# Attention with the values held in TensorE, two heads' turned weights moving, and four sample pages side by side

## The chip, the cores and the metric

The kernel runs as one program on one NeuronCore of a Trainium2 chip. The metric is the device time of an execution in microseconds, as the median of three runs.

## The reference, cut to what matters

One layer of a decoder: a projection, two groups of eight attention heads side by side, an output projection and a SwiGLU block, for a prompt of 1024 tokens and eight samples that each have 4096 earlier tokens in pages of 128. What matters here is the attention of the prompt, and the stick-breaking attention of the samples:

```python
# group A, per head: three branches over the prompt, merged by gates
p = softmax(q @ kc.T * scale + mask_c); o_cmp = p @ vc        # 63 compressed keys
o_slc = softmax(q @ k_slc.T * scale + causal) @ v_slc         # with 1024 tokens every block is selected
o_win = softmax(q @ k_win.T * scale + window) @ v_win         # the last 512 tokens
o_nsa = gates[0] * o_cmp + gates[1] * o_slc + gates[2] * o_win
# group B, per head (the prompt, and each sample over its 4096 paged rows)
z = q @ k.T * scale
log_1m = where(mask, log_sigmoid(-z), 0)
suffix = reversed_cumsum(log_1m) - log_1m
o_sb = where(mask, exp(log_sigmoid(z) + suffix), 0) @ v
```

## The kernel before

The stages are `project`, `compress`, `attend`, `decode_nsa`, `mix_out` and `swiglu`, one after another with a barrier between some of them. The diff is in `attend` and in one constant.

`attend` is written out by hand for each engine. A step is one query tile of 128 rows (`t`, 0 to 7), one of two heads (`u`) and one kind: stick-breaking (`sb`), compressed (`cmp`), selected (`sel`) or window (`win`). A body holds two heads, 64 steps in the order u, t, kind. The body runs four times: once written out, twice in a register loop (`eng.Fori(1, 3)`), once written out. A step t of `sb` and `sel` covers t + 1 key tiles, `win` at most five, `cmp` one block of 63 keys.

For each step TensorE makes the scores into one of two score banks (L1115 to L1134). For the softmax kinds VectorE takes the row maximum (L1314) and ScalarE the exponential (L1241). For `sb` VectorE copies the scores (L1318), ScalarE makes the logarithm in three steps (L1250 to L1256), GpSimd the positive part (L1088), VectorE a reversed running sum (L1328), GpSimd a difference (L1091) and ScalarE the exponential (L1262). Two steps later TensorE turns the weights, 128 x 128 at a time, into two PSUM banks (L1153), VectorE and ScalarE copy the banks out in turn (L1225, L1227). Three steps later TensorE multiplies (L1170): the turned weights are the stationary operand, 128 columns, and 64 columns of values move, 65 for the softmax kinds, whose last column is ones, so that the sum of the weights comes out beside the product. VectorE then divides by that sum, multiplies by the gate and adds into `mix` (L1335 to L1350). In step s TensorE's queue holds the scores of s, the transposes of s - 2, the product of s - 3, then the work for the samples.

The samples' stick-breaking attention is spread between these steps. While one head is worked on, SP loads the 32 key pages of sample h (128 rows of 512 numbers each, L1012) into four slots, GpSimd multiplies them by the query (L1070) and VectorE sums each head's 64 products (L1377). Meanwhile SP loads the value pages of sample h - 1 into four slots (L1018, after a wait at L1017 for a slot to come free), and TensorE multiplies them (L1190): 8 columns of weights are stationary, the page's 512 columns move, and 32 pages add up in one bank. The last sample's value pages come after the last body. SP's queue alternates key page and value page.

## Time and profile before

| | us |
|---|---|
| median of three runs | 3199.31 (3196.07 to 3200.15) |
| the profiled execution | 3171.88 |
| its span, first to last instruction | 3169.9 |
| TensorE busy in the span | 2790.5 (88%) |
| VectorE, ScalarE, GpSimd busy | 1329.0, 825.6, 865.7 |
| mean granted clock of TensorE | 0.843 of 2.4 GHz |

The span holds all stages; the changed one is about a third of it. Engines work at the same time, so their busy times don't add up. The granted clock has two levels, 1.2 and 2.4 GHz, and a mean between them says how the time is shared out.

### The profile page before, as it was taken

What the parts mean: (1) busy time and instruction counts of PE and PEld (TensorE: products, weight loads), DVE (VectorE), ACT (ScalarE), POOL (GpSimd) and SP (SyncE); (2) the same over time, 40 slices, a digit from 0 to 9 for tenths busy, and PEclk for the clock granted to TensorE, in tenths of its full rate; (3) what the DMA queues carried; (4) which work ended last, traced back from release to release, by engine and by line L of the source; (5) the groups of instructions that cost most, each with busy time, mean ns of one, the idle gap of its engine ahead of it and who ended that gap; (6) DMA issues with size and microseconds to landing.
All of it is one profiled execution on the core that took longest, in us unless ns stands there. A gap on an engine that the chain in (4) does not pass through costs nothing. (4 is left out here: it accounts for less than half of the span.)

```text
span 3169.9 us, 48300 instructions
## 1 busy us (share of the span) xinstructions
PE 2790.5 (88%) x14396; PEld 2061.5 (65%) x14396; DVE 1329.0 (42%) x2664; ACT 825.6 (26%) x1540; POOL 865.7 (27%) x909
## 2 busy tenths in 40 slices
PE   7989698949999999999999715883989999999999
PEld 6868677736755555555555203442449999999999
DVE  3562233316565656556566223332431111114444
ACT  4232233313232333333333100110221111113333
POOL 0220344215464555445455103431200000000000
PEclk9999699975596977769798955555989999999999
DMA  4233744363355454445544411213112111113200
GB/s 144 87 114 117 179 124 130 83 111 101 90 167 137 150 147 135 140 139 155 146 140 151 133 22 44 67 45 128 67 63 65 46 46 46 46 43 99 67 31 23
DMA packets 265582, 314.41 MB, mean 99 GB/s; under 512 B 58326, under 2 KB 172815, under 8 KB 265207
## 3 DMA queue, kind: packets, MB, share of 16 engines
q1 hardware_dynamic: 248423, 271.20, 29.4%
q0 software_dynamic: 16576, 40.43, 5.2%
q8 instruction: 99, 1.62, 0.2%
q14 instruction: 132, 1.08, 0.1%
q10 hardware_dynamic: 352, 0.08, 0.0%
HBM read 278.89 MB, written 37.44 MB: 100 GB/s over the span
## 5 line engine op out<-in xcount | busy, mean ns | idle before, releaser
L1070 POOL TENSOR_TENSOR late<-late 128x512 f32<-128x512 f32 x256 | 335.8, 1314 | 255.0 <-DMA late<-in_cache_sb_kv 212.5
L2036 PE MATMUL pg<-h_turned_hi,w_gu_hi 128*128 128x344 f32 x1056 | 338.4, 320 | 9.9 <-DVE h_turned_lo L2084 9.9
L2038 PE MATMUL pg<-h_turned_hi,w_gu_lo 128*128 128x344 f32 x1056 | 338.3, 320 | 0.0
L2037 PE MATMUL pg<-h_turned_lo,w_gu_hi 128*128 128x344 f32 x1056 | 338.2, 320 | 0.0
L1190 PE MATMUL decode_ps<-late,weights_dec 128*8 128x512 f32 x512 | 308.0, 704 | 8.5 <-DMA late<-in_cache_sb_kv 6.8
L1241 ACT ACTIVATE probs<-scores,minus_max 128x63 f32<-128x63 f32 (+4 forms) x192 | 109.6, 571 | 591.6 <-DVE minus_max L1314 553.3
L2162 PE MATMUL py<-w_down_hi,act_hi 128*128 128x256 f32 x792 | 225.7, 285 | 9.9 <-DVE w_down_lo L2209 9.9
L2079 DVE TENSOR_TENSOR w_gu_lo<-late,w_gu_hi 128x512 fp32r<-128x512 f32 x88 | 60.9, 692 | 402.2 <-ACT w_gu_hi L2049 402.2
L2163 PE MATMUL py<-w_down_lo,act_hi 128*128 128x256 f32 x792 | 225.1, 284 | 0.0
L2164 PE MATMUL py<-w_down_hi,act_lo 128*128 128x256 f32 x792 | 225.0, 284 | 0.0
L2145 POOL DMA_DIRECT2D out_y_prompt<-y_rows x32 | 17.4, 545 | 745.8 <-DVE y_rows L2197 745.8
L2036 PEld LDWEIGHTS pg<-h_turned_hi,w_gu_hi 128*128 128x128 f32 x1056 | 199.5, 189 | 10.1 <-issue 9.9
L2038 PEld LDWEIGHTS pg<-h_turned_hi,w_gu_lo 128*128 128x128 f32 x1056 | 199.6, 189 | 0.0
L2037 PEld LDWEIGHTS pg<-h_turned_lo,w_gu_hi 128*128 128x128 f32 x1056 | 199.1, 189 | 0.0
L1170 PE MATMUL out_ps<-v_sel_win,probs_turned 128*128 128x65 f32 (+1 forms) x1056 | 178.6, 326 | 11.6 <-DVE mix L1348 10.8
L1170 PEld LDWEIGHTS out_ps<-v_sel_win,probs_turned 128*128 128x128 f32 x1056 | 170.9, 245 | 23.3 <-issue 21.4
L831 DVE TENSOR_TENSOR rows_turned_lo<-px_c,rows_turned_hi 128x256 fp32r<-128x256 f32 x264 | 99.7, 420 | 189.5 <-ACT rows_turned_hi L782 189.5
L1377 DVE TENSOR_REDUCE z_dec<-late 128x8 f32<-128x512 f32 x256 | 169.0, 673 | 5.2 <-POOL late L1070 5.1
L2204 DVE TENSOR_TENSOR act_lo<-swiglu_act,act_hi 128x1408 fp32r<-128x1408 f32 (+1 forms) x72 | 105.9, 1471 | 149.5 <-ACT act_hi L2181 149.5
L2049 ACT ACTIVATE w_gu_hi<-late 128x512 fp32r<-128x512 f32 x88 | 55.7, 633 | 417.4 <-PE pg L2038 410.1
L1614 POOL DMA_DIRECT2D kv_sel<-in_cache_nsa_kv x144 | 84.4, 586 | 279.6 <-issue 279.6
L2162 PEld LDWEIGHTS py<-w_down_hi,act_hi 128*128 128x128 f32 x792 | 153.0, 193 | 11.2 <-issue 11.2
(289 smaller groups left out, 5743.5 us busy)
## 6 DMA issues: line engine op xcount, KB each, us to landing
late<-in_cache_sb_kv SPq DMA_DIRECT2D x512, 256.0 KB, 2.9
late<-in_w_gate_up SPq DMA_DIRECT2D x88, 256.0 KB, 2.9
late<-in_cache_nsa_kv SPq DMA_DIRECT2D x160, 128.0 KB, 3.7
late<-in_cache_nsa_kv POOLq DMA_DIRECT2D x96, 128.0 KB, 3.4
late<-in_w_down SPq DMA_DIRECT2D x4, 2816.0 KB, 11.0
w_in_raw<-in_w_in SPq DMA_DIRECT2D x40, 256.0 KB, 4.9
kv_sel<-in_cache_nsa_kv POOLq DMA_DIRECT2D x144, 32.0 KB, 2.0
x_sb<-in_x_prompt SPq DMA_DIRECT2D x8, 512.0 KB, 4.1
```

What stands on the lines that cost most here:

```text
L1070: eng.tensor_tensor(prod[:, p % NPR], kr[:, p % RING], qb[:, u], ALU.mult).then_inc(multiplied, 1)
L1170: mm = eng.matmul(O[:, 0:HD if kind == "sb" else HD + 1], l, r, start=c == 0, stop=c == tiles - 1)
L1190: eng.matmul(DB[0:NH, :], aw[:, :, NPAGE - 1 - p], vr[:, p % RING], start=p == 0, stop=p == NPAGE - 1).then_inc(v_used, 1)
L1241: eng.activation(pr[:, s % 2, 0:w], S[:, s % 2, 0:w], ACT.Exp, bias=nm[:, s:s + 1]).then_inc(exp_done, 1)
L1377: eng.tensor_reduce(zd[:, u, :, NPAGE - 1 - p], prod[:, p % NPR].rearrange("p (h d) -> p h d", h=NH), AX.X, ALU.add).then_inc(reduced, 1)
L2036: eng.matmul(pg[:, e, c, 0:CW], w_hi[:, h, j, :], hT_hi[:, k, cols], start=k == 0, stop=False)
L2037: eng.matmul(pg[:, e, c, 0:CW], w_hi[:, h, j, :], hT_lo[:, k, cols], start=False, stop=False)
L2038: mm = eng.matmul(pg[:, e, c, 0:CW], w_lo[:, h, j, :], hT_hi[:, k, cols], start=False, stop=k == KT - 1)
L2162: eng.matmul(out, a_hi[:, h, j, :], wd_hi[:, f, :], start=f == 0, stop=False)
L2163: eng.matmul(out, a_hi[:, h, j, :], wd_lo[:, f, :], start=False, stop=False)
L2164: mm = eng.matmul(out, a_lo[:, h, j, :], wd_hi[:, f, :], start=False, stop=f == NF - 1)
L2204: eng.tensor_tensor(lo, src, hi.bitcast(F32), ALU.subtract).then_inc(a_lo_done, 1)
```

## The change

- **Products.** The values become the stationary operand (64 columns) and the turned weights move. For the softmax kinds the weights of two heads stand side by side in `prT`, 256 columns, because both heads share keys and values; for `sb` each head moves its own 128. Each product fills one of two column halves of TensorE and lands in PSUM partitions 0 to 63 or 64 to 127 of the bank `O`: selected and window, or the two `sb` heads, or two query tiles of `cmp`. A batch is such a pair; a block of 16 steps (two heads, two query tiles) has five, and the three larger kinds are issued in pieces over two or three steps (`PV_AT`).
- **Output.** The result stands with its columns in the partitions, so ScalarE copies it to `oT` (`copy_out`), TensorE turns it back into one of the two banks that the transposes use (`turn_back`), and VectorE scales and adds (`finish`). The sums of the weights come from ScalarE's exponential (`accum_out` into `den`) in place of the column of ones.
- **Bank copies.** VectorE copies every third bank, ScalarE the others.
- **Samples' values.** Eight slots in place of four. Four pages go one after another to four column groups of 32 (the weights padded with zeros to 32 columns) and to PSUM partitions 0, 32, 64 and 96; each group adds up eight pages, and a matmul with 128 ones adds the four. The weights are still ready one head later, but key and value pages are spread evenly by an estimate of each step's cost (`DEC`) over 288 slots in the one sequence, the last sample's values among them.
- **Order.** No register loop: 256 steps are written out, with two heads and two query tiles alternating in a block. Page numbers are read eight at a time. Queries are loaded per block, by GpSimd's queue, which also takes the loads of the `sb` values from SP.

```diff
-        vx = sb("v_sel_win", [P, 2, TILES, KVH, HD + 1])
...
+        vx = sb("v_sel_win", [P, 2, TILES, KVH, HD])
+        qn = sb("q_nsa_hi_twice", [P, 2, 2, 2 * P], F32R)
+        qs = sb("q_sb_hi_twice", [P, 2, 2, 2 * P], F32R)
+        qn_lo = sb("q_nsa_lo", [HD, 2, 2, 2 * P], F32R)
+        qs_lo = sb("q_sb_lo", [HD, 2, 2, 2 * P], F32R)
...
-        prT = sb("probs_turned", [P, 2, TILES, P])
-        fac = sb("factor", [P, 64, 2])
...
+        SB_SLOT, EVEN_SLOT, ODD_SLOT, CMP_SLOT, SLOTS = 0, 8, 20, 33, 35
+        prT = sb("probs_turned", [P, SLOTS, 2 * P])
+        fac = sb("factor", [P, 2, 4])
+        part = sb("out_parts", [P, 2, 2, HD])
...
+        vr_low = late[:, 2048:4096].rearrange("p (r n) -> p r n", r=VRING // 2)
+        vr_high = sb("value_pages_high", [P, VRING // 2, 512])
+        value_slot = lambda p: (vr_low, vr_high)[p % VRING // 4][:, p % 4]
...
-        aw = sb("weights_dec", [P, NH, NPAGE])
+        aw = sb("weights_dec", [P, 32, NPAGE])
...
+        BLOCK = [(0, 0, "sb"), (0, 0, "cmp"), (1, 0, "cmp"), (0, 1, "cmp"), (1, 0, "sb"), (1, 1, "cmp"), (0, 0, "sel"), (1, 0, "sel"),
+                 (0, 1, "sb"), (0, 0, "win"), (1, 0, "win"), (0, 1, "sel"), (1, 1, "sb"), (1, 1, "sel"), (0, 1, "win"), (1, 1, "win")]
+        STEPS = [(N, u, 2 * k + a, kind) for N in range(NBODY) for k in range(4) for u, a, kind in BLOCK]
...
+        NBATCH = 5 * U // 16
+        PV_AT, OUT_AT = ((8,), (10, 11), (12, 13, 14), (18, 19), (20, 21, 22)), (9, 12, 15, 20, 23)
+        END = U - 16 + OUT_AT[4] + 1
...
+        PT_USES = []
+        for i in range(END):
+            PT_USES += [("out", bt) for bt, _ in at_iteration(i, OUT_AT)]
+            if 2 <= i < U + 2:
+                PT_USES += [("group", b) for b in range(G0[i - 2], G0[i - 1])]
+        bank_of = {use: n % 2 for n, use in enumerate(PT_USES)}
+        use_before = {use: PT_USES[n - 2] for n, use in enumerate(PT_USES) if n >= 2}
+
+        cost = [0.9 + 0.4 * tiles_of(kind, t) for N, u, t, kind in STEPS]
+        DEC = [[] for _ in range(END)]
+        for n in range((NH + 1) * NPAGE):
+            goal, i, total = (n + 0.5) / ((NH + 1) * NPAGE) * sum(cost), 0, cost[0]
+            while total < goal:
+                i += 1
+                total += cost[i]
+            DEC[i].append((n // NPAGE, n % NPAGE))
+        VGROUP = {6: 0, 9: 1, 13: 2, 16: 3, 20: 4, 23: 5, 27: 6, 31: 7}
+        reduced_at = lambda s: [] if s == 0 else [s - 1] if s < NPAGE - 1 else [s - 1, s]
...
-                def value_page(b, p):
-                    if not (zero(b) and p < RING):
-                        eng.wait_ge(v_used, b * NPAGE + p - RING + 1)
-                    page = eng.value_load(pt[0:1, bass.ds(b * NPAGE + p, 1)], min_val=0, max_val=NPOOL - 1)
-                    eng.dma_start(vr[:, p % RING], io["cache_sb"][bass.ds(page * P, P), 1, :]).then_inc(v_loaded[p % RING], 16)
+                def value_page(b, p, page):
+                    if b or p >= VRING:
+                        eng.wait_ge(v_used, b * NPAGE + p - VRING + 1)
+                    eng.dma_start(value_slot(p), io["cache_sb"][bass.ds(page * P, P), 1, :]).then_inc(v_loaded[p % VRING], 16)
...
+                def load_queries(blk, n):
+                    N, k = blk // 4, blk % 4
+                    dst, name, t = ((qs[0:HD], "T_hi", T_QS), (qs[HD:P], "T_hi", T_QS), (qs_lo, "T_lo", T_QS),
+                                    (qn[0:HD], "T_hi", T_QN), (qn[HD:P], "T_hi", T_QN), (qn_lo, "T_lo", T_QN))[n]
+                    src = turned_rows[name][:, t + 2 * N:t + 2 * N + 2, 2 * P * k:2 * P * (k + 1)]
+                    eng.dma_start(dst[:, blk % 2], src).then_inc(q_blocks[blk % 2], 16)
+
+                def load_keys(N):
+                    for rows, name in ((slice(0, HD), "T_hi"), (slice(HD, P), "T_lo")):
+                        eng.dma_start(ks[rows], turned_rows[name][:, T_KB + 2 * N:T_KB + 2 * N + 2, :]).then_inc(ks_loaded, 16)
+
+                def load_values(N):
+                    v = io["sb_p"].rearrange("(t p) (c h d) -> c p t h d", p=P, c=2, h=NH)[1]
+                    for u in range(2):
+                        eng.dma_start(vs[:, u], v[:, :, 2 * N + u, :]).then_inc(vs_loaded, 16)
...
+                def bank_free(use):
+                    if use in use_before:
+                        what, n = use_before[use]
+                        if what == "out":
+                            eng.wait_ge(out_done, n + 1)
                         else:
+                            eng.wait_ge(saved[saver(n)], saves(n + 1)[saver(n)])
...
+                def turn_back(bt):
+                    N, t, kind, W = batch(bt)
+                    eng.wait_ge(ot_saved, bt + 1)
+                    bank_free(("out", bt))
+                    for u in range(W // P):
+                        mm = eng.transpose(PT[:, bank_of["out", bt], u * P:(u + 1) * P], oT[:, bt % 2, u * P:(u + 1) * P], ident[:, :])
+                    mm.then_inc(out_turned, 1)
...
-                    for c in range(tiles):
-                        if kind == "cmp":
-                            l, r = prT[0:NCP, m % 2, 0, :], vcp[0:NCP, bass.ds(kv, 1), :].rearrange("p o d -> p (o d)")
-                        elif kind == "sb":
-                            l, r = prT[:, m % 2, c, :], vs[:, u, c, :]
-                        else:
-                            l, r = prT[:, m % 2, c, :], vx[:, 0 if kind == "sel" else 1, lo + c, bass.ds(kv, 1), :].rearrange("p o d -> p (o d)")
-                        mm = eng.matmul(O[:, 0:HD if kind == "sb" else HD + 1], l, r, start=c == 0, stop=c == tiles - 1)
-                    mm.then_inc(pv_done, 1)
...
+                def product(bt, piece):
+                    N, t, kind, W = batch(bt)
+                    kv, pieces = N // 2, len(PV_AT[bt % 5])
+                    if piece == 0:
+                        by_v, by_a = saves(groups_ready(bt))
+                        eng.wait_ge(saved[0], by_v)
+                        eng.wait_ge(saved[1], by_a)
+                        if bt:
+                            eng.wait_ge(ot_saved, bt)
+                        if kind == "sb":
+                            eng.wait_ge(vs_loaded, 32 * (N + 1))
+                    if kind == "cmp":
+                        for z in range(2):
+                            mm = eng.matmul(O[HD * z:HD * z + HD, 0:W], vcp[0:NCP, kv, 0:HD], prT[0:NCP, CMP_SLOT + z, :], start=True, stop=True)
+                        mm.then_inc(pv_done, 1)
+                        return
+                    count = (t + 1, t + 1 if kind == "sb" else tiles_of("win", t))
+                    for c in range((t + 1) * piece // pieces, (t + 1) * (piece + 1) // pieces):
+                        for z in range(2):
+                            if c >= count[z]:
+                                continue
+                            if kind == "sb":
+                                l, r = vs[:, z, c, :], prT[:, SB_SLOT + c, z * P:z * P + P]
+                            else:
+                                name = ("sel", "win")[z]
+                                l, r = vx[:, z, first_tile(name, t) + c, kv, :], prT[:, slot_of(name, t) + c, :]
+                            mm = eng.matmul(O[HD * z:HD * z + HD, 0:W], l, r, start=c == 0, stop=c == count[z] - 1)
+                    if piece == pieces - 1:
+                        mm.then_inc(pv_done, 1)
...
-                            eng.matmul(DB[0:NH, :], aw[:, :, NPAGE - 1 - p], vr[:, p % RING], start=p == 0, stop=p == NPAGE - 1).then_inc(v_used, 1)
...
+                    if 1 <= h <= NH and s in VGROUP:
+                        pages = [SIDE * VGROUP[s] + i for i in range(SIDE)]
+                        if pages[0] == 0:
+                            eng.wait_ge(weights_done, h)
+                        for p in pages:
+                            eng.wait_ge(v_loaded[p % VRING], h * VPER - VPER + 16 * (p // VRING) + 16)
+                        for i, p in enumerate(pages):
+                            eng.matmul(DB[32 * i:32 * i + 32, :], aw[:, :, NPAGE - 1 - p], value_slot(p), start=p < SIDE, stop=p >= NPAGE - SIDE).then_inc(v_used, 1)
...
+                for i in range(END):
+                    if i < U:
+                        scores(i)
+                    for bt, _ in at_iteration(i, OUT_AT):
+                        turn_back(bt)
+                    if 2 <= i < U + 2:
+                        transposes(i - 2)
+                    for bt, piece in at_iteration(i, PV_AT):
+                        product(bt, piece)
+                    for h, s in DEC[i]:
+                        sample(h, s)
...
+                def copy_out(bt):
+                    N, t, kind, W = batch(bt)
+                    eng.wait_ge(pv_done, bt + 1)
+                    if bt >= 2:
+                        eng.wait_ge(out_turned, bt - 1)
+                    eng.activation(oT[:, bt % 2, 0:W], O[:, 0:W], ACT.Copy).then_inc(ot_saved, 1)
+
...
-                    f, f2 = fac[:, m % U, 0:1], fac[:, m % U, 1:2]
-                    eng.reciprocal(f, O[:, HD:HD + 1])
-                    eng.drain()
-                    eng.tensor_tensor(f2, f, gates[:, t, bass.ds(h * 3 + br, 1)], ALU.mult)
-                    eng.drain()
-                    if kind == "cmp" and t == 0:
-                        eng.tensor_tensor(f2, f2, rowok[:, :], ALU.mult)
-                    mx = mix[:, t, bass.ds(h * HD, HD)]
-                    if kind == "cmp":
-                        eng.tensor_scalar(mx, o, f2, None, ALU.mult).then_inc(out_done, 1)
-                    else:
-                        eng.scalar_tensor_tensor(mx, o, f2, mx, ALU.mult, ALU.add).then_inc(out_done, 1)
...
+                def finish(bt):
+                    N, t, kind, W = batch(bt)
+                    bank = PT[:, bank_of["out", bt], 0:W]
                     if kind == "sb":
+                        eng.wait_ge(out_turned, bt + 1)
+                        eng.tensor_copy(mix[:, t, 512 + 2 * N * HD:512 + 2 * N * HD + P], bank).then_inc(out_done, 1)
                         return
+                    f4 = fac[:, bt % 2, :].rearrange("p (a b) -> p a b", a=2)
+                    eng.wait_ge(out_turned, bt + 1)
+                    if kind == "cmp":
+                        eng.reciprocal(f4, den[:, t:t + 2, :, 0])
                         eng.drain()
+                        eng.tensor_tensor(f4, f4, gates[:, t:t + 2, 6 * N:6 * N + 6:3], ALU.mult)
+                        eng.drain()
+                        if t == 0:
+                            eng.tensor_scalar(f4[:, 0, :], f4[:, 0, :], rowok[:, 0:1], None, ALU.mult)
+                            eng.drain()
+                        out = mix[:, t:t + 2, 2 * N * HD:2 * N * HD + P].rearrange("p t (u d) -> p t u d", u=2)
+                        src = bank.rearrange("p (u t d) -> p t u d", u=2, t=2)
+                        eng.tensor_tensor(out, src, f4.unsqueeze(3).broadcast_to([P, 2, 2, HD]), ALU.mult).then_inc(out_done, 1)
+                        return
+                    eng.reciprocal(f4, den[:, t, :, 1:3])
+                    eng.drain()
+                    eng.tensor_tensor(f4, f4, gates[:, t, 6 * N:6 * N + 6].rearrange("p (u b) -> p u b", u=2)[:, :, 1:3], ALU.mult)
+                    eng.drain()
+                    src = bank.rearrange("p (u b d) -> p u b d", u=2, b=2)
+                    eng.tensor_tensor(part[:, :, :, :], src, f4.unsqueeze(3).broadcast_to([P, 2, 2, HD]), ALU.mult).then_inc(out_done, 1)
+                    eng.drain()
+                    mx = mix[:, t, 2 * N * HD:2 * N * HD + P].rearrange("p (u d) -> p u d", u=2)
+                    for z in range(2):
+                        eng.tensor_tensor(mx, mx, part[:, :, z, :], ALU.add)
```

## Rows read from the trace of the kernel before

**Rows 1.** The page, the granted clock of TensorE in 40 slices, in tenths
```profile
PEclk9999699975596977769798955555989999999999
```

**Rows 2.** Busy time by stretch: PE, weight loads, VectorE, ScalarE, GpSimd, granted clock, DMA
```profile
715.00:865.00 150.00, 143.82 (x514) 105.55 (x514) 89.99 (x208) 48.71 (x97) 75.25 (x61) 0.50 0.29 86
890.00:960.00 70.00, 69.26 (x345) 38.61 (x344) 49.67 (x97) 28.41 (x43) 44.51 (x29) 1.00 0.59 174
965.00:1009.00 44.00, 43.19 (x132) 25.06 (x131) 20.48 (x60) 10.75 (x29) 14.31 (x17) 0.50 0.43 112
715.00:1770.00 1055.00, 1021.19 (x4185) 596.06 (x4185) 652.54 (x1445) 358.67 (x662) 550.46 (x432) 0.77 0.48 137
...
1770.00:1816.00 46.00, 36.63 (x72) 5.05 (x70) 1.32 (x3) 0.42 (x1) 0.00 (x0) 0.93 0.53 160
```

**Rows 3.** PE's waits in 715 to 1770 us: total, times, longest
```profile
PE turned_ps L1153 <- ACT probs L1241: 16.1, 13, 4.9
```

**Rows 4.** Busy by stretch (PE, weight loads): L1170 alone, then L1190 alone
```profile
715.00:1770.00 1055.00, 304.10 (x1760) 285.54 (x1760) 0.77 0.48 137
...
715.00:1770.00 1055.00, 274.19 (x448) 27.86 (x448) 0.77 0.48 137
```

**Rows 5.** PE's timeline at granted clock 1.00: start, duration of the run, count
```profile
1196.40 1.89 PE L1190 MATMUL decode_ps<-late,weights_dec 128*8 128x512 f32 x4
1198.22 0.29 PE L1115 MATMUL scores<-kc_prompt_hi,q_nsa_hi_twice 64*128 x1
...
1198.71 0.85 PE L1153 MATMUL turned_ps<-ident,stick_weights 128*128 128x128 f32 x6
1199.40 1.23 PE L1170 MATMUL out_ps<-v_sel_win,probs_turned 128*128 x10
1200.56 1.03 PE L1190 MATMUL decode_ps<-late,weights_dec 128*8 128x512 f32 x2
```

**Rows 6.** PE's timeline at granted clock 0.50
```profile
871.35 0.96 PE L1170 MATMUL out_ps<-v_sel_win,probs_turned 128*128 128x65 f32 x4
872.23 1.88 PE L1190 MATMUL decode_ps<-late,weights_dec 128*8 128x512 f32 x2
874.04 0.69 PE L1131 MATMUL scores<-kT_sel_win,q_nsa_hi_twice 128*128 128x384 f32 x1
```

**Rows 7.** PE's timeline before 965 us; in brackets the idle time before
```profile
962.92 0.76 PE L1153 MATMUL turned_ps<-ident,probs 128*128 128x128 f32 x5 [1.03 <-ACT probs L1241]
```

**Rows 8.** VectorE by line, 715 to 1770 us; the last row by shape
```profile
L1341 DVE TENSOR_TENSOR factor<-factor,gates 128x1 f32<-128x1 f32 x192 | 82.1, 428 | 26.9 <-issue 19.7
L1225 DVE COPY probs_turned<-turned_ps 128x512 f32<-128x512 f32 (+4 forms) x176 | 79.0, 449 | 9.7 <-PE turned_ps L1153 9.6
...
L1335 DVE COPY mix<-out_ps 128x64 f32 (+1 forms) x63 | 14.0, 223 | 32.1 <-PE out_ps L1170 31.1
...
L1374 DVE TENSOR_TENSOR logw_dec<-z_dec,decode_ps 128x256 f32<-128x256 f32 x7 | 2.9, 421 | 8.1 <-PE decode_ps L1184 8.1
```

**Rows 9.** ScalarE by line and shape, 715 to 1770 us
```profile
L1227 ACT ACTIVATE probs_turned<-turned_ps 128x256 f32<-128x256 f32 x32 | 12.1, 378 | 0.6
```

**Rows 10.** GpSimd by line, 715 to 1770 us
```profile
L1070 POOL TENSOR_TENSOR late<-late 128x512 f32<-128x512 f32 x256 | 335.8, 1314 | 255.0 <-DMA late<-in_cache_sb_kv 212.5 <-DVE z_dec L1377 40.8 <-issue 0.9
L1088 POOL TENSOR_SCALAR late<-late 128x128 f32<-128x128 f32 (+3 forms) x64 | 105.2, 1643 | 36.1 <-DVE late L1318 36.1
L1091 POOL TENSOR_TENSOR late<-late 128x128 f32<-128x128 f32 (+3 forms) x64 | 89.7, 1402 | 234.2 <-DVE late L1328 234.2
L1056 POOL DMA_DIRECT2D q_sb_hi_twice<-scratch_T_hi x12 | 7.0, 580 | 0.0
```

**Rows 11.** Line L997: count, duration in ns (least, median, most), first and last start
```profile
L997 SPq DMA_DIRECT2D v_sel_win<-out_nsa_p x2: 628/8348/16067, 677.3 to 686.1; - x2
```

**Rows 12.** SP's own waits, 715 to 1820 us
```profile
SPq L1017 <- PE decode_ps L1190: 365.6, 133, 21.3
```

**Rows 13.** Line L1170, the same columns as rows 11
```profile
L1170 PE MATMUL out_ps<-v_sb,probs_turned x576: 222/275/447, 730.1 to 1769.8; 128*128 128x64 f32 x192
```

More of the change, by code:

```diff
@@ L974, in attend @@
-        zero = lambda N: isinstance(N, int) and N == 0
-        def turns(eng, body, tail):
-            body(0, 0)
-            with eng.Fori(1, 3) as i:
-                body(i, i - 1)
-            body(3, 1)
-            for s in range(H):
-                tail(s)
+        for m in range(U):
+            N, u, t, kind = STEPS[front_of(m)]
+            G0.append(G0[-1] + (tiles_of(kind, t) + 3) // 4)
+        saver = lambda b: 0 if b % 3 == 2 else 1
+        saves = lambda b: (b // 3, b - b // 3)
@@ L1037, in tail @@
-                def tail(s):
-                    value_page(NH - 1, s)
-                    if s == 5:
-                        store_row(NH - 2)
-                turns(eng, body, tail)
+                    eng.dma_start(io["osb_s"][b:b + 1, :], orow).then_inc(row_stored, 16)
+                for h in range(NH + 1):
+                    for p0 in range(0, NPAGE, 8):
+                        key_ids = numbers(h, p0) if h < NH else None
+                        value_ids = numbers(h - 1, p0) if h else None
+                        for p in range(p0, p0 + 8):
+                            if h < NH:
+                                key_page(h, p, key_ids[p - p0])
+                            if h:
+                                value_page(h - 1, p, value_ids[p - p0])
+                            if p == 5 and h >= 2:
+                                store_row(h - 2)
@@ L1125, in scores @@
                         e = min(w, a + 512)
-                        if kind == "sb":
-                            k = ks[:, u, a:e]
-                        else:
-                            k = kT[:, 0 if kind == "sel" else 1, bass.ds(kv, 1), lo * P + a:lo * P + e].rearrange("p o c -> p (o c)")
-                        own = [x for x in edges if a <= x[0] < e]
-                        eng.matmul(S[:, s % 2, a:e], q, k, start=True, stop=False)
-                        mm = eng.matmul(S[:, s % 2, a:e], q_lo, k[0:HD], start=False, stop=not own)
@@ L1133, in scores @@
-                        for z, (at, m) in enumerate(own):
-                            mm = eng.matmul(S[:, s % 2, at:at + P], identb[:, :], masks[:, m, :], start=False, stop=z == len(own) - 1)
-                    mm.then_inc(qk_done, 1)
-                def transposes(N, m):
-                    u, t, kind, lo, tiles = BACK[m % U]
+                        k = ks[:, u, a:e] if kind == "sb" else kT[:, 0 if kind == "sel" else 1, kv, lo * P + a:lo * P + e]
+                        own = [x for x in edges if a <= x[0] < e]
@@ L1146, in transposes @@
-                    for b in range(first, G0[m % U + 1]):
-                        if not (zero(N) and b < 2 and m >= 0):
-                            eng.wait_ge(saved[b % 2], N * (G // 2) + (base + b) // 2)
-                        if kind == "cmp":
-                            eng.sem_inc(steps, 1)
-                        for c in range(4 * (b - first), min(tiles, 4 * (b - first) + 4)):
-                            w = min(P, width(BACK[m % U]) - c * P)
-                            mm = eng.transpose(PT[0:w, b % 2, (c % 4) * P:(c % 4 + 1) * P], src[:, c * P:c * P + w], ident[:, :])
-                        mm.then_inc(turned, 1)
@@ L1192, in body @@
-                def body(N, kv):
-                    for s in range(U):
-                        scores(N, kv, s)
-                        kvb = lambda m: kv if m >= 0 else (1 if isinstance(N, int) else 0)
-                        if not (zero(N) and s < 2):
-                            transposes(N, s - 2)
-                        if not (zero(N) and s < 3):
-                            product(N, kvb(s - 3), s - 3)
-                        sample(N * 2 + s // H, s % H)
-                def tail(s):
-                    if s < 2:
-                        transposes(4, s - 2)
-                    if s < 3:
-                        product(4, 1, s - 3)
-                    sample(NH, s)
```

464 lines of the change are left out of this document (224 added, 240 removed).

## The prediction, on record before the change was run

> **What bounds the kernel now.** I read the page first: its row of the granted clock falls to half in the middle of the span [rows 1]. The change touches one stage, `attend`, so everything else keeps its time. The view by stretches shows that stage: work runs from 715 to 1770 us, and a tail of 46 us follows in which only TensorE and transfers are left [rows 2]. In the 1055 us of the body PE is busy 1021, VectorE 653, GpSimd 550, ScalarE 359, so PE sets the pace. The waits confirm it: PE's own longest comes to 16 us in 13 times [rows 3]. A microsecond of PE work taken out of the body is therefore worth about a microsecond, until another engine takes over.
>
> Two lines hold half of that work [rows 4]. The products (L1170) are busy 304 us in 1760 instructions; a run's last instruction overlaps what follows by some 0.07 us (1.23 recorded, 1.16 to the next start [rows 5]), and with about 256 runs that leaves 286. The sample's value pages (L1190) are busy 274 in the body; less 10 for the same reason leaves 264. The other lines and 34 us of idleness are 1055 - 286 - 264 = 505, so 471 of work.
>
> The clock is the second thing to read. In [rows 2] the stretches 715 to 865 and 965 to 1009 run at 0.50 (1.2 GHz) although PE is busy 96% and 98% of them; 890 to 960 runs at 1.00 (2.4 GHz), and the tail has 0.93 on average, although PE is busy only 37 of its 46 us. Prices at both levels come from the timeline, from one start to the next. At 2.4 GHz [rows 5]: a value matmul of 512 columns (1198.22 - 1196.40) / 4 = 0.455 us, a product of 65 columns 1.16 / 10 = 0.116, a transpose 0.69 / 6 = 0.115. At 1.2 GHz [rows 6]: 1.81 / 2 = 0.905 and 0.88 / 4 = 0.22. At 2.4 GHz throughout, the products would be 1760 x 0.116 = 204 and the body's pages 448 x 0.455 = 204. They took 550 for 408, so the mix of clocks now costs a factor of 1.35, and the other 471 are 348 at 2.4 GHz.
>
> **The change, part by part.**
>
> *Products.* Now the turned weights are loaded (128 columns) and 64 or 65 columns of values move. After it 64 columns of values are loaded and 256 columns (two heads) or 128 move. An fp32 matmul is two instructions (880 calls, 1760 rows). The new ones: compressed 16 batches x 2 x 2 = 64 of 256 columns; stick-breaking 36 tiles x 4 pairs x 2 heads x 2 = 576 of 128; selected 36 x 4 x 2 = 288 and window 30 x 4 x 2 = 240 of 256. By columns from the 512-column row, 256 cost 0.227 and 128 cost 0.114: 14.5 + 65.7 + 65.4 + 54.5 = 200. So streamed one after another the new products cost what the old ones do, 204. All of the gain hangs on the two column halves running at the same time. No matmul of this trace writes another part of the columns than the first, so the price lies between 200 and, with each pair at the cost of its longer half, 7 + 33 + 65 = 105. I take 105.
>
> *Value pages.* 512 instructions of 0.455 are 233 one after another. Four pages side by side could take a quarter, 58. But a page's second instruction has the page's own columns and must follow its first; in the order written, page 2's first can run beside page 1's second, and so on, so four pages take 5 steps for 8: 64 x 5 x 0.455 = 146. I take that. By the Trainium skill (TensorEngine Tiling (Array Packing), Theoretical Speedup), a dimension of up to 32 gives up to four times, which is the 58 and would make the result some 110 us lower; no row here shows either.
>
> *Turning back.* 128 new transposes x 0.115 = 15.
>
> *Unchanged*: 348 at 2.4 GHz. The tail of 46 us goes, because the pages of the last sample are now spread over the whole body; their work is in the 146.
>
> So PE's work at 2.4 GHz is 105 + 146 + 15 + 348 = 614, against 204 + 233 + 348 = 785 now; without any overlap it is 200 + 233 + 15 + 348 = 796.
>
> *The clock after.* The factor can be 1.0, or stay at 1.35, or reach 1.95 (0.22 / 0.116 and 0.905 / 0.455 average to that) if 2.4 GHz is never granted. The slow stretch 715 to 865 is the one almost without pages, where short products fill PE; the tail kept 2.4 GHz on long matmuls with gaps. The change turns 1760 short instructions into 1168 long ones, which speaks for a smaller factor. Against it, the clock fell at 965 right after PE had waited 1.03 us for ScalarE [rows 7], and a faster PE waits more. I take 1.25: 614 x 1.25 = 768.
>
> *Waits.* The 34 us of idleness stay. New ones: each of the 80 batches goes PE, ScalarE copy, PE turn, VectorE, and the turned block shares two PSUM banks with the transposes, so these queue behind `finish`. That chain is 0.38 (a 256-column copy on ScalarE [rows 9]) + 0.23 (two turns) + 0.16, 0.43 and 0.42 on VectorE (reciprocal, a one-column multiply, a 256-column multiply out of PSUM [rows 8]) = 1.6 us, of which the scores and products in between hide some. Between 0 and 80 x 1.6 = 128 I take 0.5 each: 40.
>
> *The other engines.* VectorE loses the five lines of the old output step (182 us in all, 82 of them the one-column multiply that takes 0.43 on average [rows 8]) and a third of its 79 us of bank copies, and gains about 93 (48 reciprocals and multiplies, 48 products of 128x256, 64 additions, 32 copies): 653 - 182 - 26 + 93 = 538. ScalarE gains 59 bank copies and 80 of `copy_out`: 359 + 54 = 413. GpSimd keeps 336 of key products and 195 of L1088 and L1091, and issues 102 loads at about 0.58: 590 [rows 10]. The eight value loads, moved to its queue from SP's, have many short rows; the same shape of issue took 0.6 to 16 us on SP [rows 11], so at worst they add 128 there. All stay below 842, so they cost nothing by themselves, but GpSimd no longer has half its time free. SP waited 366 us for the value matmuls to free a slot [rows 12]; eight slots in place of four, freed by fours, leave it as far ahead, so I cost it at nothing. Register instructions go with the loop; they run ahead of a busy PE, nothing.
>
> *Sum.* 768 + 34 + 40 = 842 from 715 to the end of the stage, where it was 1055 + 46 + 1 = 1102: 260 less. The profiled execution took 3171.9, 27 below the median of 3199.3. 3172 - 260 = 2912, and 2939 as a median: **2940 us**.
>
> **Rivals.**
>
> *PE near full clock.* Factor 1.0: 614 + 74 = 688, 414 less, 2785. For it: the long instructions. Against it: GpSimd's 590 and VectorE's 538 in strict order would then nearly pace it.
>
> *Each change between whole and divided columns empties the array.* There are 176 product pieces and 64 page groups, so 480 changes. A product of 64 columns is recorded at 0.275 [rows 13] where the next starts after 0.116; the 0.16 between is what an empty array would show. 480 x 0.16 = 77, so 919, and 3016. For it: the pieces are short, one to three per block and batch. Against it: no row, since nothing divides columns now. The Trainium skill (TensorEngine Tiling (Array Packing), Key Properties) states that changing the tiling mode drains TensorE; by that rule this rival holds.
>
> *The halves do not run together (the other side).* Place: products and pages. The work is then 796, above the 785 of now. At today's factor it is 796 x 1.35 + 74 = 1149, 47 more: 3246; at 1.25 it is 1069, 33 less: 3166. At 1.35 it decides as soon as overlap hides under 35 of the 433 us, since (1102 - 74) / 1.35 = 761. For it: the two instructions of one call always follow each other, and moving data for two halves must be read at once. Against it: nothing in the trace. This is also the case in which the change does not do what it says.
>
> *The clock stays at 1.2 GHz.* 614 x 1.95 + 74 = 1271, 169 more: 3368. For it: 715 to 865. Against it: every later stretch with pages comes back to 2.4 GHz.
>
> **How the numbers follow.** Forecast (overlap, factor 1.15 to 1.35, own range 2880 to 3000) 0.42; emptied array 0.16; near full clock 0.17; no overlap 0.18, of which a third is still faster; half clock 0.07. Faster by over 0.2%, about what a measurement of this kernel tells from no change: 0.42 + 0.16 + 0.17 + 0.06 = 0.81; within it 0.03; slower 0.16. The range of 2785 to 3200 leaves out the half clock, the slower part of no overlap and a little below: 0.2.
>
> **What would show it.** Right: two product matmuls of one piece starting within 0.02 us of each other or at half their stream; pages at some 2.3 us per group of four at 2.4 GHz; the body ending near 1557 with no tail; PE's granted clock above 0.8 there. Wrong: page instructions still 0.45 apart (no overlap); gaps of 0.1 to 0.2 us at the edges of each piece (emptying); 0.50 over long stretches; long PE waits for VectorE or ScalarE at the transposes after `turn_back`, or GpSimd busy over 90%, which would put the chain in place of PE's work.

## The result, and the profile after

| | before | after |
|---|---|---|
| median of four runs each | 3197.69 us | 3082.79 us (3075.28 to 3089.52) |
| ratio to before, 95% interval | | 0.9646 (0.9615 to 0.9677) |
| profiled execution | 3171.9 us | 3089.5 us |
| first to last matmul of `attend` | 714.5 to 1816.2, 1102 us | 703.7 to 1730.5, 1027 us |
| PE idle in it, mean granted clock | 43 us, 0.77 | 165 us, 0.67 |

The kernel is 3.5% faster: 115 us, where 260 were forecast. The two profiled executions are only 82 us apart, since that of the kernel before was 26 us below its median and that of the changed kernel 7 us above. Outside the stage the time changed by 8 us: the stage begins 11 us earlier, and what follows it takes 3 us longer. The clock row of the profile's page shows where to look:

```profile
PEclk9999799985567667667567655556999999999999
```

Where [rows 1] had 6 to 9 in the middle of the stage, this row has 5 to 7. The view by stretches (columns as in [rows 2]), the whole stage first and then its parts:

```profile
705.00:1730.00 1025.00, 860.20 (x3789) 456.64 (x3788) 574.61 (x985) 413.04 (x994) 576.39 (x486) 0.67 0.50 149
...
705.00:841.00 136.00, 116.89 (x412) 65.53 (x411) 81.19 (x151) 56.51 (x158) 91.11 (x85) 0.50 0.44 127
841.00:1400.00 559.00, 464.99 (x2132) 245.60 (x2132) 327.72 (x553) 229.09 (x545) 341.38 (x287) 0.71 0.56 168
1400.00:1730.00 330.00, 278.32 (x1248) 145.51 (x1247) 165.70 (x282) 127.44 (x291) 143.91 (x115) 0.68 0.43 127
```

PE is busy 860 us where it was 1058, and its clock is lower. Busy time times the mean clock is an estimate of the work in microseconds at 2.4 GHz: 860 x 0.67 = 576 against 1058 x 0.77 = 815. So some 239 us of work are gone, more than the forecast's 171. What answers to [rows 4], products (L1224) and pages (L1245):

```profile
L1224 PE MATMUL out_ps<-probs_turned,v_sel_win 128*64 128x256 f32 x528 | 105.7, 503 | 0.0
L1224 PE MATMUL out_ps<-probs_turned,v_sb 128*64 128x128 f32 x576 | 67.6, 387 | 1.1 <-issue 0.7 <-ACT probs_turned L1277 0.2
L1245 PE MATMUL decode_ps<-value_pages_high,weights_dec 128*32 128x512 f32 x256 | 57.9, 993 | 0.0
L1245 PE MATMUL decode_ps<-late,weights_dec 128*32 128x512 f32 x256 | 50.9, 878 | 0.0
```

The timeline at 2.4 GHz, which answers to [rows 5], shows how:

```profile
1132.45 1.08 PE L1224 MATMUL out_ps<-probs_turned,v_sel_win 128*64 128x256 f32 x8
...
1133.47 0.50 PE L1160 MATMUL scores<-kT_sel_win,q_nsa_hi_twice 128*128 128x512 f32 x1
...
1136.35 1.12 PE L1245 MATMUL decode_ps<-value_pages_high,weights_dec 128*32 128x512 f32 x8
...
1137.40 0.49 PE L1160 MATMUL scores<-kT_sel_win,q_nsa_hi_twice 128*128 128x512 f32 x1
```

Eight product instructions of 256 columns take 1.02 us, 0.128 each, where one after another at the 0.227 of the forecast would be 1.82. Eight page instructions take 1.05, 0.13 each for 0.455: the four pages run side by side, and both instructions of a call do. What PE waited for, against the single row in [rows 3]:

```profile
PE turned_ps L1187 <- DVE out_parts L1416: 81.9, 28, 8.6
PE turned_ps L1195 <- ACT late L1320: 24.9, 25, 3.4
PE decode_ps L1236 <- ACT late L1334: 18.9, 7, 5.4
PE turned_ps L1187 <- DVE mix L1409: 12.2, 13, 2.0
```

Three of these four rows are the new chain: turned output, `finish`, a bank free again. Its longest wait in the timelines of three engines:

```profile
1138.78 2.02 DVE L1388 TENSOR_TENSOR_SCAN late<-late 128x896 f32<-128x896 f32 x1 [2.36 <-ACT late L1308]
...
1139.35 0.60 PE L1187 MATMUL turned_ps<-ident,probs 128*128 128x128 f32 x4
...
1140.72 1.85 DVE L1449 TENSOR_REDUCE z_dec<-late 128x8 f32<-128x512 f32 x3
1142.49 1.08 DVE L1373 TENSOR_REDUCE minus_max<-scores 128x1 f32<-128x896 f32 x1
...
1143.41 2.08 POOL L1122 TENSOR_TENSOR late<-late 128x896 f32<-128x896 f32 x1
...
1143.73 4.22 DVE L1413 TENSOR_TENSOR factor<-factor,gates 128x4 f32<-128x4 f32 x1
...
1145.44 2.48 POOL L1096 TENSOR_TENSOR late<-late 128x512 f32<-128x512 f32 x2
...
1148.02 0.42 DVE L1416 TENSOR_TENSOR out_parts<-turned_ps,factor 128x256 f32<-128x256 f32 x1
1148.50 0.90 PE L1187 MATMUL turned_ps<-ident,probs 128*128 128x128 f32 x3 [8.55 <-DVE out_parts L1416]
```

VectorE takes 4.22 us to multiply four columns, and ends as GpSimd's three tensor instructions end (1143.41 to 1147.92). PE waits 8.55 us for the bank behind it. The first 3.5 us of that wait lie ahead of `finish`, while VectorE works through a scan, three reductions and a row maximum.

### The profile page after: what moved, and what is told of

The parts are those of the page before. It is cut to its first block and busy times, and to the rows that moved or that the text cites. A ratio compares the mean times of both kernels' runs of the same rounds, so it can differ in the third digit from the quotient of the medians.

```text
span 3087.5 us, 43599 instructions
## 1 busy us (share of the span) xinstructions
PE 2598.0 (84%) x13932; PEld 1918.4 (62%) x13932; DVE 1250.4 (40%) x2201; ACT 879.9 (28%) x1871; POOL 891.7 (29%) x957
## 5 line engine op out<-in xcount | busy, mean ns | idle before, releaser
L1096 POOL TENSOR_TENSOR late<-late 128x512 f32<-128x512 f32 x256 | 322.6, 1269 | 142.9 <-DVE z_dec L1449 93.4
L1187 PE MATMUL turned_ps<-ident,probs 128*128 128x128 f32 (+1 forms) x592 | 143.2, 361 | 100.4 <-DVE out_parts L1416 81.9
L1292 ACT ACTIVATE probs<-scores,minus_max 128x63 f32<-128x63 f32 (+8 forms) x192 | 109.7, 571 | 394.6 <-DVE minus_max L1373 381.4
L1373 DVE TENSOR_REDUCE minus_max<-scores 128x1 f32<-128x63 f32 (+8 forms) x192 | 103.6, 540 | 181.0 <-PE scores L1163 144.3
L1187 PEld LDWEIGHTS turned_ps<-ident,probs 128*128 128x128 f32 (+1 forms) x592 | 93.1, 183 | 111.6 <-DVE out_parts L1416 74.6
L736 PE MATMUL ph_c<-rows_turned_hi,w_cmp_hi 128*128 128x512 f32 (+1 forms) x288 | 125.9, 437 | 37.6 <-DVE rows_turned_lo L829 37.6
```

The costliest lines, as they stand in the source:

```text
L736: eng.matmul(out, w1_hi[:, kk, half, jj, :], x_hi, start=step == 0, stop=False)
L1096: eng.tensor_tensor(prod[:, p % NPR], kr[:, p % RING], qb[:, h % 2], ALU.mult).then_inc(multiplied, 1)
L1187: mm = eng.transpose(PT[0:w, bank, (c % 4) * P:(c % 4 + 1) * P], src[:, c * P:c * P + w], ident[:, :])
L1292: eng.activation(pr[:, f % 2, 0:w], S[:, f % 2, 0:w], ACT.Exp, bias=nm[:, f % 8:f % 8 + 1], accum_out=den[:, t, u, br:br + 1]).then_inc(ex ...
```

## The experiments

Two things had moved: the clock (0.77 to 0.67) and the idle time (43 to 165 us). **Theory A**: the waits pull the clock down, so taking waits away gives both back. **Theory B**: the clock follows how much work the array has; the change took work away and the clock went with it. Theories C and D stand in the expectations. Each ratio is to the kernel before on the same chip. The other columns are from one profiled execution: the stage goes from the first to the last matmul of `attend`, and PE's busy time is taken over whole microseconds, so that a row can miss its stage by 1 or 2 us.

| kernel | stage us | PE busy | PE idle | clock | ratio (95%) |
|---|---|---|---|---|---|
| before | 1102 | 1058 | 43 | 0.77 | 1 |
| after | 1027 | 860 | 165 | 0.67 | 0.9646 (0.9615 to 0.9677) |
| after, no gate multiply | 989 | 855 | 133 | 0.68 | 0.9594 (0.9536 to 0.9653) |
| after, factors on GpSimd | 996 | 860 | 134 | 0.66 | 0.9605 (0.9545 to 0.9665) |
| after, pages in turn | 1093 | 931 | 161 | 0.80 | 0.9918 (0.9890 to 0.9946) |
| after, halves in turn | 1016 | 856 | 159 | 0.68 | 0.9694 (0.9636 to 0.9751) |
| after, one dense matmul a step | 1011 | 841 | 169 | 0.76 | 0.9641 (0.9593 to 0.9688) |
| after, three | 1035 | 884 | 151 | 0.85 | 0.9682 (0.9635 to 0.9729) |
| factors on GpSimd, one dense | 992 | 836 | 155 | 0.76 | 0.9548 (0.9502 to 0.9593) |
| the same, dense in the waits | 998 | 846 | 151 | 0.78 | 0.9579 (0.9527 to 0.9630) |
| before, one dense | 1052 | 1007 | 44 | 0.86 | 0.9755 (0.9709 to 0.9801) |
| before, pages alone, ring of 4 | 1282 | 1156 | 125 | 0.51 | 1.0488 (1.0441 to 1.0534) |
| the same, three dense | 1229 | 1008 | 220 | 0.78 | 1.0356 (1.0304 to 1.0409) |
| before, pages alone, ring of 8 | 1180 | 1145 | 34 | 0.51 | 1.0161 (1.0093 to 1.0229) |
| the same, one dense | 1125 | 1048 | 76 | 0.63 | 0.9956 (0.9920 to 0.9992) |
| the same, two dense | 1063 | 964 | 98 | 0.77 | 0.9824 (0.9747 to 0.9901) |

**Fewer waits.** The first run drops the multiply by the gates, here and in the branch for `cmp`; its outputs lack the gates:

```diff
                     eng.reciprocal(f4, den[:, t, :, 1:3])
                     eng.drain()
-                    eng.tensor_tensor(f4, f4, gates[...][:, :, 1:3], ALU.mult)
-                    eng.drain()
```

> Leaves out the multiplication of the reciprocal by the gates in finish (48 of VectorE's small SBUF-to-SBUF multiplies, 49 us busy, up to 4.2 us each); the outputs lack the gates. Theory A (PE's waits pull the clock down): the 94 us that PE waits for VectorE at the two shared banks fall to about 40, the stage's mean granted clock rises from 0.67 to 0.72 or more, and the time falls by 100 to 130 us. Theory B (the clock follows how much long streaming work PE has, not the waits): the waits fall the same way, the clock stays at 0.67, and the time falls by 30 to 50 us.

The second keeps the result and makes the factor on GpSimd, a step ahead:

```diff
+                    eng.tensor_tensor(f4, d4, minus1[...], ALU.pow)
+                    eng.drain()
+                    mm = eng.tensor_tensor(f4, f4, g4, ALU.mult)
```

> GpSimd works out gate / sum for a batch one step before VectorE needs it (a power of -1 and a multiply on 4 columns), so finish is one multiply out of PSUM before the bank is free; same results. Theory A: waits at the banks fall by 50 or more, the clock rises to 0.72 or more, 80 to 130 us faster than the changed kernel. Theory B: 30 to 50 us faster at a clock of 0.67.

The bank wait halves in both (81.9 to 41.6 and 42.3). This is its row without the multiply:

```profile
PE turned_ps L1187 <- DVE out_parts L1412: 41.6, 19, 4.3
```

In the whole stage 31 us of idleness went, and the clock stayed (0.68, 0.66) where theory A had 0.72 or more. By the ratios 0.5 and 0.4 points came back, about 15 us each, but the intervals overlap that of the change, so this gain is not shown. Theory A falls.

**The parts of the overlap.** Pages of a group one after another in the same 32 columns:

```diff
-    eng.matmul(DB[32 * i:32 * i + 32, :], aw[:, :, NPAGE - 1 - p], value_slot(p), ...)
+    eng.matmul(DB[0:32, :], aw[:, :, NPAGE - 1 - p], value_slot(p), ...)
```

> Puts the four value pages of a group back into one column group, one after another; all else as in the changed kernel. Their work at 2.4 GHz goes from 68 to 233 us. Theory A: the clock stays near 0.67 and the time rises by 165 x 1.54 = 254, less some 30 of waits that the longer work covers: 200 to 250 us. Theory B: the long work brings the clock back to 0.75 or above in the stage and the time rises by 100 us or less.

```profile
704.00:1796.00 1092.00, 931.19 (x3791) 447.12 (x3791) 566.28 (x985) 411.15 (x994) 576.21 (x486) 0.80 0.46 140
```

The pages cost 0.45 each again, 512 x (0.45 - 0.13) = 164 us more work at 2.4 GHz, but the stage is only 66 us longer: the clock rose to 0.80 with 161 us of waits still there. It is also the change without its pages, and gains 0.8%.

Halves of a product one after the other:

```diff
-    for c in range(...):
-        for z in range(2):
+    for z in range(2):
+        for c in range(...):
```

> Issues each piece's matmuls for the first column half, then those for the second, where the changed kernel alternates; the same instructions and results, but only neighbours at the turn can overlap. Work at 2.4 GHz rises by 26 (stick-breaking) and up to 40 (window) us. Theory A: 66 x 1.54 = 100 us slower at most, 60 to 100. Theory B: the clock rises a little with it, 20 to 50 us slower. If the halves hardly overlapped in the first place, no change.

No difference beyond the intervals. The records show why: the second half starts beside the first all the same, and a 256-column product averages 0.15 us at 2.4 GHz in both kernels (128 columns: 0.091 for 0.069).

**Useless work.** If B is right, work that nobody uses must raise the clock and cost little. One dense matmul (the whole array, 512 columns) ahead of each step's scores, into the bank that they overwrite; then three, by `range(3)`:

```diff
+    for z in range(1):
+        eng.matmul(S[:, f % 2, 0:512], identb[:, :], cmask[...], start=True, stop=True)
```

> The changed kernel with one more matmul in each of the 256 steps of the stage, ahead of the step's scores: 512 columns of 16-bit values over the whole array, into the bank that the scores then overwrite. It computes nothing that is used. One costs about 0.22 us at 2.4 GHz and 0.43 at 1.2, by the scores of 512 columns, 56 or 110 us in all. Theory B (the granted clock of the stage follows how much the array streams; the three cheaper parts took work away and with it the clock): the stage's mean granted clock rises from 0.67 to about 0.71, which gives back most of the price: stage 1020 to 1050 us against 1022, ratio 0.962 to 0.975 against the changed kernel's 0.965. Theory C (the clock is set by something that the added work doesn't change, the breaks between short batches, say): the clock stays at 0.67, the 56 us cost 84, stage about 1106, ratio 0.99.

> As the run with one dense matmul per step, with three of them: 168 us of work at 2.4 GHz that is not used. Theory B: the clock rises to about 0.80, as it did with the pages in turn, and the stage takes about 1090 us (744 us of work over 0.80, and 160 idle), ratio 0.985 to 0.995. Theory C: the clock stays at 0.67, 250 us more, stage about 1270 us, ratio 1.04.

With three, by stretches:

```profile
701.00:1736.00 1035.00, 884.06 (x4560) 445.78 (x4560) 564.59 (x985) 410.73 (x994) 576.26 (x486) 0.85 0.50 148
```

For 56 and 168 us of added work, one costs nothing that can be measured and three about 0.4 points, with intervals that overlap; the clock rose to 0.76 and 0.85. Theory C had 0.99 and 1.04. The waits did not go (169 and 151 us), so they are not what holds the clock. The same single matmul in the kernel before:

> The kernel before, with one dense matmul ahead of each step's scores and nothing else. Theory B: its clock rises from 0.77 to about 0.85, 815 us of work and 56 more over 0.85 is 1025, with 43 idle a stage of 1068 against 1102, ratio 0.99. Theory C: clock 0.77, 56 us cost 73, ratio 1.02.

```profile
715.00:1766.00 1051.00, 1006.99 (x4434) 573.53 (x4510) 642.21 (x1448) 359.56 (x664) 552.27 (x432) 0.86 0.51 144
```

56 us of work that computes nothing made the stage 50 us shorter and the kernel 2.4% faster, more than the expected 1%.

**The pages alone.** The kernel before, with four pages side by side and nothing else of the change:

```diff
+    for p in range(b, b + 4):
+        eng.matmul(DB[32 * (p - b):32 * (p - b) + 32, :], aw[:, :, NPAGE - 1 - p], vr[:, p % RING], ...)
```

> The kernel before with one part of the change alone: four value pages of a sample in a row, each in its own 32 columns of the array, on the same ring of four pages; the prompt's attention, its order and its loads as before. The products keep 64 or 65 columns over the whole array. The pages' work falls from 307 us by about 220. Theory B: the clock of the stage falls from 0.77 to about 0.67 as in the changed kernel, since as much work has gone; busy time 1058 x 0.77 = 815 us less 236 is 579, over 0.67 is 864, with 34 to 80 us idle a stage of 900 to 945 us against 1102, ratio 0.937 to 0.951: no slower than the whole change, which would mean that the rest of the change gained nothing. Theory C (the changed kernel's short batches and their waits brought the clock down): the clock stays at 0.77 here, 579 / 0.77 = 752, stage 790 to 830 us, ratio 0.90 to 0.915.

> The kernel before with the pages side by side alone, and three dense matmuls ahead of each step's scores, 168 us of work at 2.4 GHz that nothing uses. Theory B (the pages alone were slower than before only because the clock fell to 1.2 GHz, 98% of the stage): the clock comes back to about 0.85; 588 us of work and 168 more over 0.85 is 889, with 100 to 125 us idle a stage of about 1000 us, ratio 0.96 to 0.975, faster with the useless work than without by some 280 us. Rival D (the page's waits for their data or the blocked load queue made it slow): the clock stays near 0.51 and the stage grows by 330 us, ratio 1.15.

Both forecasts missed: 4.9% slower at 0.51, and with the clock brought back to 0.78 still 3.6% slower. So the clock was not all of it. GpSimd's wait for key pages pointed to the ring of four: SP holds one queue, and key pages stood in it behind value pages that waited for a whole group to be used. That row with the ring of four:

```profile
POOL late L1068 <- DMA late<-in_cache_sb_kv: 477.5, 139, 34.6
```

With the ring of eight of the change added:

> The kernel before with the pages side by side, and now also with the ring of eight value pages of the changed kernel; the prompt's attention as before. In the run without the larger ring GpSimd waited 478 us for key pages, which stood on the load queue behind value pages that waited for their slots (212 us in the kernel before). If both that and the clock made it slow, the two part here. The late keys gone: PE idle falls from 125 us to 40 to 80. The clock: theory B gives 579 us of work (815 less 236) over a clock that follows the streaming; at 0.67 as in the changed kernel 864, stage 905 to 945, ratio 0.937 to 0.951; at 0.51 as in the run with the small ring 1135, stage about 1190, ratio 1.025. Products of 64 columns over the whole array are shorter than those of the changed kernel, so the lower clock is the likelier, 0.55 to 0.6, ratio about 1.0.

```profile
POOL late L1071 <- DMA late<-in_cache_sb_kv: 40.5, 4, 32.6
...
713.00:1892.00 1179.00, 1145.40 (x4256) 788.17 (x4256) 643.70 (x1448) 358.39 (x663) 538.53 (x432) 0.51 0.43 129
```

The late keys are gone (478 to 41 us) and PE is busy 97% of the stage. With 34 us of waits left and about 230 us less work at 2.4 GHz the stage is 78 us longer, because it ran at 1.2 GHz for 98% of its time. It also limits theory B: 1145 x 0.51 = 584 us of work is as much as the changed kernel's 576, which ran at 0.67, so the amount of work alone does not set the clock. Giving work back:

> As the run before it, with one dense matmul ahead of each step's scores, 56 us at 2.4 GHz. Theory B: the clock comes back to 0.70 to 0.75: 635 us of work over it is 850 to 907, with 50 idle a stage of 900 to 960, ratio 0.937 to 0.955, which would be no slower than the whole change. If the rest of the change (values stationary, the unrolled order) is what made it faster: the ratio stays at 1.0 or above.

> As the run before it with two dense matmuls per step, 112 us. Theory B: clock about 0.80, 691 us over it is 864 and 50 idle, stage about 915, ratio 0.94.

The clock came up more slowly than expected (0.63, in a profiled execution 19 us above its median, and 0.77), and idle time with it (76, 98), so 0.9956 and 0.9824 stand for the forecast 0.95 and 0.94. B's direction held, its sizes did not. With two useless matmuls a step to bring back the clock of the kernel before, pages side by side are worth 1.8%; one useless matmul without them gave 2.4%, and the intervals overlap. The change with its pages in turn gains 0.8%, so neither half reaches the change's 3.5% by itself. How the rest divides over the products, the order of the steps and the loads is not shown; no run takes these apart.

**Both remedies together.** The factors on GpSimd and one dense matmul per step; then two matmuls behind the scores, ahead of the bank wait, in the 160 narrow steps:

```diff
                     mm.then_inc(qk_done, 1)
+                    dense(f)
...
+                    a = 512 if width(kind, t) <= 512 else 1024
+                    for z in range(2 if a == 512 else 0):
+                        eng.matmul(S[:, f % 2, a:1024], identb[:, :], cmask[...], start=True, stop=True)
```

> The run with the factors on GpSimd, and one dense matmul ahead of each step's scores as in that run. Theory B (the clock follows how much the array streams, and waits are paid beside it): both gains add: 573 us of work and 56 more over a clock of 0.755, 134 us idle, stage about 967 us, ratio about 0.951. Theory C (the clock isn't changed by added work) is refuted by now; if the gains don't add (the fewer waits and the higher clock buy the same thing), ratio 0.96.

> As the run before it, but with the dense matmuls behind the step's scores, ahead of the point where TensorE waits for the bank of the turned weights, and only in the 160 steps whose scores fill one bank: two each, into the other bank, 70 us at 2.4 GHz. Theory B: the clock rises to about 0.78, and part of the added work lies in time that was idle: 643 us over 0.78 is 824, with 110 to 134 idle a stage of 935 to 960 us, ratio 0.942 to 0.950. If place does not matter: as the run before it, 0.951; if only the wide steps need the work, the clock stays near 0.70 and the ratio is 0.97.

The first is the best kernel of the study, 0.9548, and its interval lies below that of the change. That it beats the factors alone (0.9605) is not shown: the intervals overlap, and the stage is 992 against 996. Work put ahead of the wait did not shorten it (idle 151).

## Why the prediction failed

In its own terms, the stage was to be 614 x 1.25 + 74 = 842. With the products and pages that the trace shows, and the prediction's 15 and 348 kept, the work is 128 + 68 + 15 + 348 = 559; busy time over it is 860 / 559 = 1.54, and 559 x 1.54 + 165 = 1026. From 842: work -55 x 1.25 = -69; clock 559 x 0.29 = +162; waits +91.

*The clock factor is the step that failed.* The prediction took 1.25, below today's 1.35, because "1760 short instructions" became "1168 long ones". It had the other reading in front of it: the stretch "almost without pages" of [rows 2] ran at 0.50 with PE busy 96%. The pages' long matmuls were the work that held the clock up, and the change took 70% of it out (233 to 68 us at 2.4 GHz). Putting them back in turn raised 0.67 to 0.80, and the runs with the pages alone made the whole stage like that stretch, 0.51. The rival "the clock stays at 1.2 GHz" had 0.07; it was the neighbour of what happened (66% of the stage at 1.2 GHz, before 46%). The Trainium skill (TensorE: Matmul & The Clock Gate, Part 1: The HAM clock gate) says that "the default state is throttled, and activity releases the throttle"; these runs agree, with 0.67, 0.76 and 0.85 for none, one and three useless matmuls. But a busy PE was not enough: with the pages alone and the ring of eight it was busy from 1579.1 to 1741.8 us, 163 us without a break, at 1.2 GHz. What exactly the clock follows stays open: 164 us of pages in turn gave 0.80, 168 us of matmuls spread over all steps 0.85, and nearly equal work ran at 0.67 and 0.51.

*Waits, second.* 40 were allowed for the new chain between 0 and 128. The rows for the turned banks shown above, with 3.3 from a smaller one, give 81.9 + 24.9 + 12.2 + 3.3 = 122, near the upper bound. The mis-sized term is the small multiply: 0.43 a piece from [rows 8], measured 1.24 on average (0.16 to 4.22). Taking it away halved the bank wait. For part of what is left the sum has no term: `finish` queues behind VectorE's other work, 3.5 us of it in the longest wait shown above.

*Work.* Pages: 146 forecast, 68 measured. The "5 steps for 8" were wrong; a page's second instruction does not hold up the other pages, and a group takes 1.05 us where 2.3 were named. Products: 105 forecast, 128 measured (528 instructions at 0.15, 576 at 0.069, 64 at 0.145). So the -55 is -78 and +23, two errors that partly cancel. The two halves start 0.007 us apart and a pair of 256 columns takes 0.21, so the overlap is as forecast; the rest is the next point.

*The array emptied at each change* was given 0.16 as a rival of its own. It happens, at a smaller price. In the records at 2.4 GHz a transpose takes 0.109 from start to start within a run and 0.203 as the last ahead of a product (in the kernel before, where products use all columns, 0.109 there too; these are medians). The last instruction of a pair of 256 columns takes 0.209 ahead of the next pair and 0.309 ahead of whole-array work. So a change costs 0.09 to 0.10, not 0.16: 480 changes are some 48 us, partly within the 128 and 68 above, and more than paid for by the pages. The Trainium skill (TensorEngine Tiling (Array Packing), Key Properties) says that changing the tiling mode drains TensorE; the trace agrees, with 0.09 to 0.10 us a change. That there was no row for it was wrong: in the kernel before the last product ahead of a page (8 columns of weights) takes 0.205 where others take 0.112, and a page's last instruction ahead of scores 0.52 where others take 0.44. Some 180 runs of pages there, where the changed kernel has 64, paid such a price twice each, so most of the 480 stand in place of changes that were there before. That the two have one cause is not shown.

*Right:* the halves and pages run together, so "no overlap" is refuted; the tail is gone; ScalarE 413 us (forecast 413), GpSimd 576 (590), VectorE 575 (538). GpSimd's loads and SP's ring cost nothing visible. *Wrong:* the end at 1557 (it is 1730), and a clock above 0.8.

Where the gain went, against the kernel before: 785 x 1.35 + 43 = 1103. Removing 226 of work at the old clock is worth 305; the lower clock took 559 x 0.19 = 106 of it, the new waits 122, and 77 are left, the stage's 75.

## What to carry to other kernels

Before counting a microsecond of TensorE work as a microsecond, find out which matmuls of the stage hold its clock up: here the wasteful ones did, and removing them alone made the kernel 1.6% slower (1.0093 to 1.0229). A dense matmul that computes nothing, one per step, is a cheap test of that (here 2.4% on the kernel before, nothing on the changed one). When two engines share a bank in strict order, price the smallest instruction of the chain by its worst case beside the other engines, not by its mean, and add the work that stands ahead of the chain on its engine.

## What was not expected of the hardware

A VectorE multiply of 128x4 between two SBUF operands took between 0.16 and 4.22 us; in the long case it ended with GpSimd's tensor instructions, while the multiply out of PSUM behind it took 0.42:

```profile
L1413 DVE TENSOR_TENSOR factor<-factor,gates x32: 164/1041/4218, 735.1 to 1726.5; 128x4 f32<-128x4 f32 x32
```

Of the 32, 29 end 18 to 32 ns after a GpSimd tensor instruction does; the other three, with none running, took 0.16. That the multiply waits for GpSimd is read from these times; no run took GpSimd's work away. GpSimd itself takes 1.06 us for a power of 128x4 and 0.22 for the multiply:

```profile
L1114 POOL TENSOR_TENSOR factor<-weight_sums,minus_one 128x4 f32<-128x4 f32 x48 | 50.8, 1058 | 0.0
L1116 POOL TENSOR_TENSOR factor<-factor,gates 128x4 f32<-128x4 f32 x48 | 10.4, 216 | 64.7 <-issue 47.4 <-DVE z_dec L1467 16.7
```

Written one half after the other, product matmuls of different column halves still overlapped: in a piece of eight instructions of 256 columns the second half's first started 0.014 us after the first half's. And the clock can stay at 1.2 GHz for 98% of a stage in which PE is busy 97% of the time.
